# ScalarE's share of the mixer reordered, four decay banks, late gate weights, and the first tap of the K, V and Q tiles on VectorE

## The chip, the core and the metric

The kernel runs on one core of one Trainium2 chip. The metric is the device time of one launch in microseconds (us). It is written engine by engine: TensorE (PE in the profile), VectorE (DVE), ScalarE (ACT), GpSimd (POOL, only masks at the start) and the DMA queue of SyncE (SP) each run their own fixed list of instructions, and semaphores tie them together. An engine executes its list in order: a wait in it holds up everything behind it.

## The reference

Two layers, each of them a feed-forward block, a mixer, a second feed-forward block and a norm, on 512 tokens of width 1024 in float32. The change is in the mixer alone:

```python
def gated_deltanet_group(h, conv_w, a_log, dt_bias, out_g):
    qkv = jax.nn.silu(causal_depthwise_conv(h[..., Q0:Z0], conv_w))   # 4 taps, 12 tiles of 128 channels
    ...
    q = l2_normalize(qkv[:, :, 0]) * (GDN_HEAD_DIM ** -0.5)
    k = l2_normalize(qkv[:, :, 1])
    v = qkv[:, :, 2]
    ...
    g = -jnp.exp(a_log) * jax.nn.softplus(a + dt_bias)
    beta = jax.nn.sigmoid(b)
    o = chunk_gated_delta_rule(q, k, v, g, beta)    # 4 heads; decay exp(gc_i - gc_j); a triangular solve
    o = o * lax.rsqrt(jnp.mean(o * o, -1, keepdims=True) + NORM_EPS) * out_g
    return o * jax.nn.silu(z)

def conformer_conv_group(h, dw_w, dw_b, ln_g, ln_b):
    glu = h[..., G0:G0 + CONV_WIDTH] * jax.nn.sigmoid(h[..., G0 + CONV_WIDTH:IN_COLS])
    u = causal_depthwise_conv(glu, dw_w) + dw_b     # 31 taps, 4 tiles of 128 channels
    return jax.nn.silu(layer_norm(u, ln_g, ln_b))
```

## The kernel before

All large products keep float32 accuracy by splitting both operands: ScalarE rounds each 128x1024 piece of weights (`high`, L866, writes `wh`), VectorE subtracts to get the rest (`weight_low`, L1229, writes `wl`), and TensorE does three matmuls for one (L446 to L448). Such a piece is called a unit; a unit is 24 matmuls of 512 columns. There are four slots of weights: unit r+4 is loaded and prepared once unit r is done, `refill(r)` being VectorE's part.

The mixer of a layer goes in four stages.

1. **Input tiles.** Units 0 to 7 are the gated convolution's input. Units 8 to 19 are the twelve tiles of K (0 to 3), V (4 to 7) and Q (8 to 11). VectorE takes a tile out of its bank (`unit_out`, L1438, writes `pre`), which lets TensorE use the bank again three units on. ScalarE does the first of the four taps (`first_tap`, L1003, writes `cacc`), VectorE the other three (L1468), ScalarE the silu (`activate`, L1009) and, for K and Q, the square (L1012). Between these VectorE puts taps of the 31-tap convolution (`conv_taps`, L1393; 124 of them, wherever it would wait), shared out by the table `taps`. Inside this stage lie the gates: cumulated sums of g on TensorE, written to the bank `stat`; the squared norms of K; and the decay matrices, two matmuls (L637, L639) for each head into one of three banks, which ScalarE turns by an exponential into `Dm` (`decay`, L1025) and scales (`decay_scaled`, L1034).
2. **System.** TensorE forms K K for each head (L656) once its Q tile has left the bank, and Q K (L664) once VectorE has taken K K out (`system`, L1510). VectorE multiplies both by `Dm`. TensorE turns `Um` (L675) and sums the squares of Q (L614, one column each), ScalarE copies to `Tm`.
3. **Levels.** Six steps of a triangular inverse, for two pairs of heads each: TensorE L715, VectorE `pm` (L1536), TensorE L724, VectorE `Tm` (L1549), TensorE transposes (L733), ScalarE `Um` (L1099). In levels 1 to 4 TensorE and ScalarE also turn and scale V and K. VectorE fills in convolution taps.
4. **Chunks.** Four steps of a recurrence over the tokens, each of them a chain TensorE, ScalarE, TensorE, VectorE. The four gate units 20 to 23 (z) are cut into 32 pieces of 3 matmuls (`z_tiles`) that TensorE does in between. With them goes the layer norm of the convolution: the last taps, token sums (L453, `u`), the mean taken off (L1587), squares (L1120), token sums (L453, `glu`), a root, the factor spread over a bank (L474, `rcol`), the product (L1629), silu and split (L1130, L1133, L1634). Then the output units can start (`mix_out`).

## Time and profile before

| | |
|---|---|
| median of 3 runs | 2227.7 us (2221.02 to 2229.23) |
| the profiled execution's own time | 2227.2 us |
| its span, first to last instruction | 2225.5 us |
| busy: TensorE, VectorE, ScalarE | 2131.2, 1205.4, 720.2 us |
| mean granted clock of TensorE | 0.957 |

The profile has a page (busy times, the span in slices, the chain that ended last) and views that are read from the trace: waits (which instruction waited for which, in total), the timeline of an engine, and windows. All times of a timeline are counted from the span's start. Matmuls are pipelined, so TensorE counts as busy wherever it has work; how fast it works is told by the granted clock, 1.00 being full. Layer 0's mixer lies at about 412 to 697 us, layer 1's at 1504 to 1792; the second repeats the first 1092.2 us later to within a few hundredths until its end.

### The profile page before, as it was taken

To read this page: it belongs to the slowest core of one execution; us is meant where nothing else is said; L and a number is where in the kernel's file an instruction comes from. 1 tells how busy PE (TensorE), PEld (TensorE's weight loads), DVE (VectorE), ACT (ScalarE), POOL (GpSimd) and SP (SyncE) were. 2 spreads that over 40 slices of the span, in tenths; PEclk is the share of its full clock that TensorE was granted. 3 is DMA by queue.
4 is the path that set the end of the run, shared out by engine and by line. 5 is a ranking of instruction groups with operands and counts; after the bars stand their busy time and mean duration, and the time that the engine had idled before them with its cause. 6 is when DMAs were issued, how large, how long until landed. Compare 5 with 4: busy or idle time off the path is not lost.

```text
span 2225.5 us, 26379 instructions
## 1 busy us (share of the span) xinstructions
PE 2131.2 (96%) x10120; PEld 1788.6 (80%) x10120; DVE 1205.4 (54%) x1657; ACT 720.2 (32%) x998; POOL 5.9 (0%) x27
## 2 busy tenths in 40 slices
PE   7999999997998999999999999999979899999997
PEld 6888887786987788888788888877778778888886
DVE  5555423885764754542365553358768546555323
ACT  4222223354324422222342222234533343222222
POOL 1000000000000000000000000000000000000000
PEclk9999999997999999999999999999969799999997
DMA  5333333321002233333233333323200123333320
GB/s 159 102 94 94 97 96 91 86 76 38 1 19 76 74 96 99 99 87 98 80 95 95 94 92 97 100 66 100 67 20 1 38 68 95 94 94 94 102 78 38
DMA packets 345791, 177.53 MB, mean 80 GB/s; under 512 B 8338, under 2 KB 344692, under 8 KB 345716
## 3 DMA queue, kind: packets, MB, share of 16 engines
q1 hardware_dynamic: 344058, 176.34, 27.8%
q8 instruction: 50, 0.82, 0.2%
q10 hardware_dynamic: 1658, 0.16, 0.1%
q14 instruction: 25, 0.20, 0.0%
HBM read 174.38 MB, written 2.10 MB: 79 GB/s over the span
## 4 chain that ended last, share of the span: by engine, by line
PE 91%; DVE 5%; ACT 2%; issue 1%; DMA 0%; SPq 0%; DVEq 0%; ACTq 0%
PE res L446 24%; PE res L448 24%; PE res L447 24%; PE pq L715 2%; PE pq L724 2%; PE stat L453 2%; PE res L510 1%; DVE u L1393 1%; PE res L511 1%; PE pq L446 1%; PE res L514 1%; PE pq L448 1%; PE pq L447 1%; PE res L733 1%; PE bc L474 1%
## 5 line engine op out<-in xcount | busy, mean ns | idle before, releaser
L866 ACT ACTIVATE wh<-raw 128x1024 fp32r<-128x1024 f32 (+1 forms) x336 | 347.9, 1038 | 1036.3 <-PE res L448 1014.0
L446 PE MATMUL res<-xh,wh 128*128 128x512 f32 x1576 | 623.6, 396 | 5.3 <-DVE xl L1243 3.0
L448 PE MATMUL res<-xh,wl 128*128 128x512 f32 x1576 | 616.7, 391 | 0.0
L447 PE MATMUL res<-xl,wh 128*128 128x512 f32 x1576 | 616.5, 391 | 0.0
L1229 DVE TENSOR_TENSOR wl<-raw,wh 128x1024 fp32r<-128x1024 f32 (+1 forms) x336 | 401.5, 1197 | 392.2 <-ACT wh L866 391.7
L446 PEld LDWEIGHTS res<-xh,wh 128*128 128x128 f32 x1576 | 298.5, 189 | 68.7 <-ACT Um L1099 2.7
L448 PEld LDWEIGHTS res<-xh,wl 128*128 128x128 f32 x1576 | 297.7, 189 | 63.2
L447 PEld LDWEIGHTS res<-xl,wh 128*128 128x128 f32 x1576 | 298.4, 189 | 61.9 <-issue 1.4
L446 PE MATMUL res<-hh,wh 128*128 128x512 f32 x704 | 273.9, 389 | 0.0
L447 PE MATMUL res<-hl,wh 128*128 128x512 f32 x704 | 273.9, 389 | 0.0
L448 PE MATMUL res<-hh,wl 128*128 128x512 f32 x704 | 273.9, 389 | 0.0
L1318 DVE TENSOR_TENSOR us<-res,rs 128x512 f32<-128x512 f32 x84 | 58.0, 690 | 237.0 <-PE res L448 237.0
L1393 DVE SCALAR_TENSOR_TENSOR u<-glu,call,u 128x512 f32<-128x512 f32 x240 | 169.6, 744 | 0.3
L447 PEld LDWEIGHTS res<-hl,wh 128*128 128x128 f32 x704 | 132.1, 188 | 27.6
L448 PEld LDWEIGHTS res<-hh,wl 128*128 128x128 f32 x704 | 132.1, 188 | 27.4
L446 PEld LDWEIGHTS res<-hh,wh 128*128 128x128 f32 x704 | 132.1, 188 | 27.3
L1321 DVE TENSOR_TENSOR hf<-gs,us 128x512 f32<-128x512 f32 x88 | 61.0, 693 | 81.0 <-ACT gs L944 81.0
L1314 DVE TENSOR_TENSOR gs<-res,rs 128x512 f32<-128x512 f32 x84 | 58.0, 691 | 47.7 <-PE res L448 42.7
L1468 DVE SCALAR_TENSOR_TENSOR cacc<-pre,call,cacc 128x512 f32<-128x512 f32 x72 | 53.8, 747 | 32.5 <-ACT cacc L1003 30.2
L1323 DVE TENSOR_TENSOR hl<-hf,hh 128x512 f32 (+1 forms) x88 | 61.0, 693 | 8.7
L510 PE MATMUL res<-xh,wh 128*128 128x512 f32 x120 | 53.5, 446 | 11.4 <-ACT xh L887 11.4
L944 ACT ACTIVATE gs<-gs 128x512 f32<-128x512 f32 x88 | 54.1, 615 | 8.3 <-DVE gs L1314 8.2
(281 smaller groups left out, 1974.1 us busy)
## 6 DMA issues: line engine op xcount, KB each, us to landing
raw<-in_ffn_w_in SPq DMA_DIRECT2D x176, 512.0 KB, 3.8
raw<-in_ffn_w_out SPq DMA_DIRECT2D x64, 448.0 KB, 3.6
raw<-in_mix_w_in SPq DMA_DIRECT2D x48, 512.0 KB, 3.9
raw<-in_ffn_w_out SPq DMA_DIRECT2D x32, 512.0 KB, 3.8
raw<-in_mix_w_out SPq DMA_DIRECT2D x16, 512.0 KB, 3.8
xin<-in_x SPq DMA_DIRECT2D x4, 512.0 KB, 5.2
out_dram<-xin SPq DMA_DIRECT2D x4, 512.0 KB, 4.0
crows<-in_cm_dw_w ACTq DMA_DIRECT2D x1, 62.0 KB
```

The lines of the kernel that those rows point to most:

```text
L446: pe.matmul(bank, wh[:, slot, j, :], hi, start=first, stop=False)
L447: pe.matmul(bank, wh[:, slot, j, :], lo, start=False, stop=False)
L448: return pe.matmul(bank, wl[:, slot, j, :], hi, start=False, stop=last)
L510: pe.matmul(banks[n], wh[:, n, k, :], xh[:, k, :], start=k == 0, stop=False)
L866: act.activation(wh[:, slot, 0:nk, :], raw[:, slot, 0:nk, :], ACT.Copy).then_inc(hi_full, 1)
L944: act.activation(gs[:, odd, :], gs[:, odd, :], ACT.Silu).then_inc(silu_done, 1)
L1229: dve.tensor_tensor(wl[:, slot, 0:nk, :], raw[:, slot, 0:nk, :], wh[:, slot, 0:nk, :].bitcast(F32), ALU.subtract).then_inc(lo_full, 1)
L1314: dve.tensor_tensor(gs[:, odd, :], in_bank(unit_bank(r, 2 * f, l)), rs[:], ALU.mult).then_inc(gate_scaled, 1)
L1318: dve.tensor_tensor(us[:, odd, :], in_bank(unit_bank(r + 1, 2 * f, l)), rs[:], ALU.mult).then_inc(pair_free, 1)
L1321: ps.link(dve.tensor_tensor(hf[:], gs[:, odd, :], us[:, odd, :], ALU.mult))
L1323: dve.tensor_tensor(hl[:, p, :], hf[:], hh[:, p, :].bitcast(F32), ALU.subtract).then_inc(h_ready, 1)
L1393: ins = dve.scalar_tensor_tensor(u[:, t, :], src, w, u[:, t, :], ALU.mult, ALU.add)
```

## The change

The first tap goes from ScalarE to VectorE, as a plain product, and ScalarE's silu of a tile moves one tile later in its list. The gate sums get a copy in SBUF (`sums`), made by VectorE behind tile 6, so that `stat` is free to be a fourth decay bank; all four decays are then issued together, behind unit 17. The root of K's norms goes from ScalarE's tile 8 to its tile 7. The weights of the four gate units are prepared in levels 0 to 3 and not in tiles 8 to 11. Two of the four mean subtractions and six of the last eight gate pieces move.

```diff
+    sums = at("gate_sums", [P, 64], F32, o_gate + 128 * len(GN))
@@ TensorE
-                    bank = three[h % 3]
+                    bank = turned[h]
...
-                mixer_units(16, 17)
-                decays(0)
-                decays(1)
-                mixer_units(17, 18)
-                decays(2)
-                mixer_units(18, 19)
-                pe.wait_ge(d_exp, l * H + 1)
-                decays(3)
-                mixer_units(19, 20)
+                mixer_units(16, 18)
+
+                pe.wait_ge(sums_out, l + 1)
+                for h in range(H):
+                    decays(h)
+                mixer_units(18, 20)
...
-                z_tiles(4)
                 for t in range(CT):
                     pe.wait_ge(usq_ready, l * CT + t + 1)
                     mm = token_sums(glu[:, t, PADC:], first=t == 0, last=t == CT - 1)
                 mm.then_inc(vsum_full, 1)
-                z_tiles(4)
+                z_tiles(2)
                 pe.wait_ge(udiag, l + 1)
                 spread_column(rcol).then_inc(uvbc_full, 1)
+                z_tiles(6)
@@ ScalarE
                     n = r - 2 * CT
-                    first_tap(n)
+                    if n:
+                        activate(n - 1)
...
-                    high(MBASE + r + SLOTS, r % SLOTS, 8, l)
+                    if n < 2 * H:
+                        high(MBASE + r + SLOTS, r % SLOTS, 8, l)
...
-                    activate(n)
-                    if n == 3:
+                    if n == 4:
                         softplus()
-                    if n == 8:
-                        act.wait_ge(l2_full, l + 1)
-                        act.wait_ge(gc_full, l + 1)
-                        act.activation(gt["ss"][:, 0:16], stat[:, 128:144], ACT.Sqrt,
+                    if n == 7:
+                        act.wait_ge(sums_out, l + 1)
+                        act.activation(gt["ss"][:, 0:16], sums[:, 32:48], ACT.Sqrt,
                                        bias=eps[:, 0:1]).then_inc(l2_root, 1)
...
+                    if n == 9:
...
                         for h in range(H):
                             decay(h)
-                    if n == 9:
+                    if n == 10:
                         decay_scaled(0)
                         decay_scaled(1)
-                    if n == 10:
+                    if n == 11:
                         decay_scaled(2)
                         decay_scaled(3)
+                activate(3 * H - 1)
...
                 for n in range(6):
+                    if n < H:
+                        high(MBASE + Z_U + n, n, 8, l)
@@ VectorE
                     unit_out(r, pre[:, PADG:])
-                    conv_taps(first)
-                    dve.wait_ge(tap0_ready, l * 3 * H + n + 1)
+                    dve.wait_ge(mix_free, l * MIX_IN_U + r + 1)
+                    if n >= 2:
+                        dve.wait_ge(act_kvqz, l * 4 * H + n - 1)
...
+                        if k == 0:
+                            mark = st.done(dve.tensor_scalar(cacc[:, n % 2, :], pre[:, 0:T], w, None, ALU.mult))
+                            conv_taps(first)
+                            continue
...
+                            elif n < 2 * H:
+                                refill(r)
                             else:
-                                refill(r)
+                                conv_taps(1)
...
-                taps = [(1, 1, 1), (1, 1, 1), (1, 1, 0), (1, 1, 1),
-                        (1, 1, 1), (1, 1, 0), (1, 0, 0), (1, 0, 0),
-                        (1, 1, 0), (1, 1, 1), (1, 1, 1), (1, 1, 0)]
+                taps = [(1, 1, 1), (1, 1, 1), (1, 0, 0), (1, 1, 0),
+                        (1, 1, 0), (1, 0, 0), (1, 0, 0), (1, 0, 0),
+                        (1, 1, 0), (1, 1, 1), (1, 1, 1), (1, 0, 0)]
...
+                    if n == 6:
+                        dve.wait_ge(gc_full, l + 1)
+                        dve.tensor_copy(sums[:], stat[:, 96:160]).then_inc(sums_out, 1)
-                    if n == 9:
+                    if n == 8:
                         dve.wait_ge(l2_root, l + 1)
...
-                        conv_taps(2)
+                        conv_taps((3, 2)[g])
+                    if n < H:
+                        weight_low(MBASE + Z_U + n, n, 8, l)
...
-                        conv_taps((2, 3)[g])
+                        conv_taps((3 if n >= H else 2, 2)[g])
...
                     if c == 3:
                         o_sum(1)
                         refill(Z_U + 1)
-                        dve.wait_ge(mubc_full, l + 1)
-                        for t in range(CT):
+                        for t in range(2, CT):
                             dve.tensor_tensor(u[:, t, :], u[:, t, :], bc[:, :], ALU.subtract).then_inc(uc_ready, 1)
...
                     if c == 2:
                         o_sum(0)
                         z_unit(1)
+                        dve.wait_ge(mubc_full, l + 1)
+                        for t in range(2):
+                            dve.tensor_tensor(u[:, t, :], u[:, t, :], bc[:, :], ALU.subtract).then_inc(uc_ready, 1)
```

The first place is ScalarE's list in the mixer around tile 8, from the root of K's norms (`gate_ss`) on. Before:

```order
L1060 ACT_TABLE_LOAD
L1060 ACTIVATE gate_ss<-stat,eps 128x16
L1062 ACT_TABLE_LOAD
L1062 ACTIVATE gate_egc<-stat 128x16
L1063 ACTIVATE gate_egl<-stat 128x16
L1064 ACTIVATE gate_ekd<-stat 128x16
L1025 ACTIVATE Dm<-pq 128x512 x2
L1025 ACTIVATE Dm<-bc 128x512
L1025 ACTIVATE Dm<-pq 128x512
L1003 ACTIVATE cacc<-pre,call 128x512
L866 ACTIVATE wh<-raw 128x1024
L1009 ACT_TABLE_LOAD
```

And now:

```order
L1054 ACTIVATE gate_ss<-gate_sums,eps 128x16
L1002 ACT_TABLE_LOAD
L1002 ACTIVATE vT<-cacc 128x512
L1002 ACTIVATE qT<-cacc 128x512
L1005 ACTIVATE ksqQ<-qT 128x512
L1057 ACT_TABLE_LOAD
L1057 ACTIVATE gate_egc<-gate_sums 128x16
L1058 ACTIVATE gate_egl<-gate_sums 128x16
L1059 ACTIVATE gate_ekd<-gate_sums 128x16
L1018 ACTIVATE Dm<-pq 128x512 x2
L1018 ACTIVATE Dm<-bc 128x512
L1018 ACTIVATE Dm<-stat 128x512
```

The tap row `cacc<-pre,call` of tile 9 stood behind the root, two table loads and the exponentials (three small ones for the gates, four for the decays); now no row of ScalarE writes `cacc`, the root stands alone ahead of the last V tile's silu (`vT`), and the mixer's list has one table load more in each layer.

The second place is VectorE's list in level 1, from the `pm` of the first pair of heads to the `Tm` of the second and what follows it (`u` rows are convolution taps). Before:

```order
L1536 TENSOR_TENSOR pm<-pq,lmask 128x512
L1393 SCALAR_TENSOR_TENSOR u<-glu,call,u 128x512 x2
L1536 TENSOR_TENSOR pm<-pq,lmask 128x512
L1393 SCALAR_TENSOR_TENSOR u<-glu,call,u 128x512 x2
L1549 TENSOR_TENSOR Tm<-Tm,pq 128x128x4
L1393 SCALAR_TENSOR_TENSOR u<-glu,call,u 128x512 x2
L1549 TENSOR_TENSOR Tm<-Tm,pq 128x128x4
L1393 SCALAR_TENSOR_TENSOR u<-glu,call,u 128x512 x3
```

The same stretch now:

```order
L1541 TENSOR_TENSOR pm<-pq,lmask 128x512
L1391 SCALAR_TENSOR_TENSOR u<-glu,call,u 128x512 x3
L1541 TENSOR_TENSOR pm<-pq,lmask 128x512
L1391 SCALAR_TENSOR_TENSOR u<-glu,call,u 128x512 x2
L1227 TENSOR_TENSOR wl<-raw,wh 128x1024
L1556 TENSOR_TENSOR Tm<-Tm,pq 128x128x4
L1391 SCALAR_TENSOR_TENSOR u<-glu,call,u 128x512 x2
L1556 TENSOR_TENSOR Tm<-Tm,pq 128x128x4
L1391 SCALAR_TENSOR_TENSOR u<-glu,call,u 128x512 x2
```

Between the first `pm` and the second `Tm` stand one tap and one weight row more; behind it one tap less.

## Rows read from the trace of the kernel before

**Rows 1.** The page: the span, and each engine's busy time.

```profile
span 2225.5 us, 26379 instructions
PE 2131.2 (96%) x10120; PEld 1788.6 (80%) x10120; DVE 1205.4 (54%) x1657; ACT 720.2 (32%) x998; POOL 5.9 (0%) x27
```

**Rows 2.** Waits, both layers: who waited for whom, total us, times, longest.

```profile
DVE cacc L1468 <- ACT cacc L1003: 30.2, 8, 7.5
...
PE res L656 <- DVE pre L1438: 13.2, 2, 6.6
PE res L446 <- DVE loc L1634: 13.2, 2, 6.6
...
PE res L664 <- ACT qT L1009: 10.9, 2, 5.5
```

**Rows 3.** Timeline of TensorE in the system stage, layer 0: start, us, instruction, [idle before].

```profile
517.89 2.89 PE L656 MATMUL res<-kT 128*128 128x128 f32 x24
527.37 2.07 PE L656 MATMUL res<-kT 128*128 128x128 f32 x8 [6.59 <-DVE pre L1438]
534.90 3.75 PE L664 MATMUL res<-qT,kT 128*128 128x128 f32 x16 [5.45 <-ACT qT L1009]
...
544.57 1.84 PE L614 MATMUL stat<-ones,ksqQ 128*128 128x1 f32 x16
...
547.59 0.75 PE L715 MATMUL pq<-Tm,Bm 128*128 128x64 f32 x3 [0.69 <-ACT Tm L1076]
```

**Rows 4.** Timeline of ScalarE, layer 0: two unit ends, and tile 8.

```profile
428.70 1.06 ACT L866 ACTIVATE wh<-raw 128x1024 fp32r<-128x1024 f32 x1 [2.30 <-PE res L448]
434.14 1.06 ACT L866 ACTIVATE wh<-raw 128x1024 fp32r<-128x1024 f32 x1 [4.38 <-PE res L448]
...
504.39 1.28 ACT L1060 ACT_TABLE_LOAD   x1
...
512.61 0.60 ACT L1025 ACTIVATE Dm<-pq 128x512 f32<-128x512 f32 x1 [3.53 <-PE pq L639]
```

**Rows 5.** Timeline of VectorE, layer 0: input tiles, and the start of the system.

```profile
421.49 1.00 DVE L1389 TENSOR_SCALAR u<-glu,call 128x512 f32<-128x512 f32 x2
...
432.60 4.06 DVE L1393 SCALAR_TENSOR_TENSOR u<-glu,call,u 128x512 f32<-128x512 f32 x6
...
513.85 0.75 DVE L1468 SCALAR_TENSOR_TENSOR cacc<-pre,call,cacc 128x512 f32<-128x512 f32 x1 [7.49 <-ACT cacc L1003]
...
526.63 0.68 DVE L1438 TENSOR_TENSOR pre<-res,rs 128x512 f32<-128x512 f32 x1
...
534.07 0.68 DVE L1510 TENSOR_TENSOR Bm<-res,Dm 128x512 f32<-128x512 f32 x1
```

**Rows 6.** Timeline of VectorE: the first `pm` of levels 0, 1 and 5.

```profile
551.15 0.69 DVE L1536 TENSOR_TENSOR pm<-pq,lmask 128x512 f32<-128x512 f32 x1 [4.81 <-PE pq L715]
...
566.64 0.69 DVE L1536 TENSOR_TENSOR pm<-pq,lmask 128x512 f32<-128x512 f32 x1 [2.57 <-PE pq L715]
...
607.18 0.69 DVE L1536 TENSOR_TENSOR pm<-pq,lmask 128x512 f32<-128x512 f32 x1 [1.32 <-PE pq L715]
```

**Rows 7.** Windows: stretch, busy times, then PEclk (granted clock), DMA share, GB/s.

```profile
535.00:541.00 6.00, 6.00 (x28) 5.92 (x29) 5.18 (x11) 1.07 (x2) 0.00 (x0) 0.50 0.30 87
548.00:564.00 16.00, 16.00 (x77) 16.00 (x77) 8.73 (x14) 0.90 (x1) 0.00 (x0) 0.50 0.00 1
...
1759.00:1766.00 7.00, 7.00 (x28) 6.13 (x28) 0.75 (x4) 1.17 (x3) 0.00 (x0) 0.54 0.01 2
```

**Rows 8.** Timeline at the end of the chunks, layer 0, three engines.

```profile
654.86 0.69 DVE L1576 TENSOR_TENSOR Xd<-pq,gate_egc 128x512 f32<-128x512 f32 x1 [0.57 <-PE pq L759]
...
663.62 2.17 ACT L1120 ACTIVATE glu<-u 128x512 f32<-128x512 f32 x4
...
665.13 3.63 PE L453 MATMUL stat<-ones,glu 128*128 128x1 f32 x32
...
671.75 0.69 DVE L1438 TENSOR_TENSOR zT<-res,rs 128x512 f32<-128x512 f32 x1 [2.30 <-PE res L448]
```

More of the change, by code:

```diff
@@ L628, in _ @@
                 pe.matmul(stat[:, 112:128], ones[:], gt["g"][:, 0:16], start=True, stop=True)
-                pe.matmul(stat[:, 160:176], lowst[:], gt["g"][:, 0:16], start=True, stop=True).then_inc(gc_full, 1)
+                pe.matmul(stat[:, 144:160], lowst[:], gt["g"][:, 0:16], start=True, stop=True).then_inc(gc_full, 1)
                 def decays(h):
-                    bank = three[h % 3]
+                    bank = turned[h]
                     if h == 0:
@@ L998, in _ @@
                 row_out(2, 1, l)
-                def first_tap(n):
-                    w0 = C_QKV + (1, 2, 0)[n // H] * H + n % H
-                    act.wait_ge(mix_free, l * MIX_IN_U + 2 * CT + n + 1)
-                    act.activation(cacc[:, n % 2, :], pre[:, 0:T], ACT.Copy,
-                                   scale=call[:, l, w0:w0 + 1]).then_inc(tap0_ready, 1)
                 def activate(n):
@@ L1024, in decay @@
                     act.wait_ge(e_full, l * H + h + 1)
-                    act.activation(Dm[:, h], three[h % 3].rearrange("p (c t) -> p c t", c=NC),
+                    act.activation(Dm[:, h], turned[h].rearrange("p (c t) -> p c t", c=NC),
                                    ACT.Exp).then_inc(d_exp, 1)
@@ L1460, in qkv @@
                     unit_out(r, pre[:, PADG:])
-                    conv_taps(first)
-                    dve.wait_ge(tap0_ready, l * 3 * H + n + 1)
-                    mark = 0
-                    for k in range(1, GTAPS):
+                    dve.wait_ge(mix_free, l * MIX_IN_U + r + 1)
+                    if n >= 2:
+                        dve.wait_ge(act_kvqz, l * 4 * H + n - 1)
+                    for k in range(GTAPS):
                         w = call[:, l, C_QKV + k * 3 * H + which * H + n % H:C_QKV + k * 3 * H + which * H + n % H + 1]
-                        if k > 1:
-                            st.need(mark)
+                        if k == 0:
+                            mark = st.done(dve.tensor_scalar(cacc[:, n % 2, :], pre[:, 0:T], w, None, ALU.mult))
+                            conv_taps(first)
+                            continue
+                        st.need(mark)
                         ins = dve.scalar_tensor_tensor(cacc[:, n % 2, :], pre[:, k:k + T], w, cacc[:, n % 2, :],
@@ L1531, in _ @@
                 scores(H - 1)
+                dve.wait_ge(br_ready, l + 1)
+                dve.wait_ge(ekd_ready, l + 1)
+                dve.tensor_tensor(gt["kd"][:, 0:16], gt["br"][:, 0:16], gt["ekd"][:, 0:16],
+                                  ALU.mult).then_inc(kd_ready, 1)
                 conv_taps(2)
```

21 lines of the change are left out of this document (9 added, 12 removed).

## The prediction

> **What bounds the kernel now.** The page first [rows 1]: TensorE is busy 96% of the span, so only what stands in TensorE's way, or slows its clock, is worth anything; VectorE at 54% and ScalarE at 32% matter only where TensorE waits for them. The waits come next [rows 2]: TensorE stands 13.2 us for VectorE's tile `pre` and 10.9 us for the silu `qT`, in two waits each, so once in each layer, and 13.2 us for `loc` at the end of the mixer. VectorE stands 30.2 us for ScalarE's first tap. Third, the timelines. TensorE finishes unit 19 and the K products of three heads by 520.8, then stands 6.59 us, does eight matmuls and stands 5.45 us [rows 3]. What is late is VectorE: its wait of 7.49 us for the first tap of tile 9 ends at 513.85, tile 11 leaves its bank at 526.63, the system starts at 534.07 [rows 5]. What held ScalarE is in rows 4: the root's table load at 504.39, then the fourth decay, which had no bank until the first was read (3.53 us), and only then the tap. Fourth, the windows [rows 7]: the granted clock is 0.50 (1.2 GHz) in 535 to 541, behind the idle stretch, and again in 548 to 564, level 0, behind two bursts of one-column matmuls, the second at 544.57 [rows 3].
>
> **The first tap on VectorE and the end of the tap wait.** Durations of VectorE overlap by some 0.09 us: six three-operand taps take 4.06, so 0.66 each; two tensor-scalar products take 1.00, so 0.46 each [rows 5]; a tensor-tensor of 0.69 counts 0.60; an instruction that needs the one just ahead starts 0.13 later. The new first tap is such a product of the same shape, 0.46. Its bounds are 0.46 and 0.66, and I take 0.46, the same form. TensorE is not slowed in the tiles: everything up to unit 17 runs as before, and it needs nothing from VectorE that is younger than two or three tiles. So unit 19 still ends at 517.9 [rows 3]. A unit takes 5.44, the distance of two passes that wait for unit ends [rows 4], and as all decays now stand ahead of unit 18, that one ends at 512.5. VectorE is at tile 10 by then and waits for it. Tile 10 is 0.73 (take out, result needed), 0.46, and seven operations of 0.66: 5.8, so tile 11 leaves its bank at 518.3. Tile 11 is 0.73 + 0.46 + five operations of 0.66 or 0.79, 3.4 in all: 4.6. The system starts at 522.9 and not at 534.07, **11.1 us earlier**. ScalarE keeps up: unit 17 ends at 502.7 (512.5 less a unit and some 4.3 for four decays, each a unit's fifth), the decays end by 506.9 and their exponentials by 509; the silu and square of tile 10 end at 519.0, the last eight scalings, 0.3 each, at 521.4, and the third head needs them only at 525.6. The bound below is unit 19's end plus 4.6, 522.5; the bound above 524.9, with 0.2 more for each of the ten remaining operations. TensorE's idle stretch shrinks from 6.59 + 5.45 to some 2.3 us.
>
> **One table load more.** It is 1.28 us long [rows 4] and stands between the root and the silu of tile 7. ScalarE is through with it at about 495.6, and that silu waits for VectorE until 497.5: I count 0. Were that cover gone, it would be 1.28 in each layer, 2.6 together.
> The Trainium skill (ScalarE: Activation LUTs, "What ACT_TABLE_LOAD costs") speaks against the change here: a switch costs 2.66 us with its drain, 5.3 us for two. By the page the sum below would be 2220.5 if nothing covered it. The row agrees with the load itself (1.28 us) and shows nothing of a drain.
>
> **The system stage.** Between 534.07 and level 0 at 547.59 lie 13.5 us [rows 3, 5], partly at 1.2 GHz. At 2.4 GHz eight matmuls of 128 columns take 0.9 and not the 1.9 of half of 3.75. From the system's start VectorE's list then sets the pace to the second Q K product, turned tile 1 ends at 5.6, a burst of one-column matmuls at 7.3, the fourth Q K at 8.2, a turned tile at 8.7, the second burst (1.7) at 10.4, the last turned tile at 10.9, and ScalarE's copy of it and the wait of 0.69 [rows 3] make 11.6: **1.9 us less**. Lower bound 0.
>
> **The levels.** `pm` of level 1 to `pm` of level 5 is 40.54 us, 10.13 a level [rows 6], and TensorE sets it: VectorE has idle time ahead of each `pm` (1.32). Now VectorE has from the first `pm` to the end of the second `Tm` 0.60 + 3 taps + 0.60 + 2 taps + 1.13 (a weight pass) + 0.60 + 2 taps + 0.69 = 8.3, taps at 0.66. Then TensorE transposes the second pair (0.9) and multiplies for the next level (1.9): 11.1. So VectorE becomes the bound in levels 1 to 3 and each costs 1.0 more; level 4, with an extra tap and no weights, is 7.8 + 2.8 = 10.6, 0.5 more; in level 5 the way to the end grows from 6.5 to 7.8, 1.3 more. Level 0, 15.5 us from `pm` to `pm` [rows 6], is slow enough at 1.2 GHz to hide it all. Sum **4.7 us more**; bounds 0 (if taps slip into waits) and 4.7 + 1.0.
>
> **The chunks.** The convolution's 124 taps are given out by tables: ahead of the chunks 22 with its own input, 27 in the tiles (23 by the table, 4 in place of refills; before 28), 2 behind the system, 56 in the levels (before 54), so 107 (before 106), then 14 in the first two steps, so the last burst, on which the token sums wait, is 3 taps and not 4: **0.7 less**. At their end it turns: two mean subtractions stand ahead of the fourth `Xd`. VectorE had 0.57 of idle time there [rows 8] and now is 0.55 late. TensorE does its 2 pieces by 663.0 and then waits for the squares, the first of which is ready at 664.2 + 0.6 [rows 8], where before it did four more pieces until 665.13. From the sums' end (3.5 us later, 668.3) eight pieces (5.44) and a spread (0.9) follow before the last gate tile can leave its bank, and that tile stands in VectorE's list ahead of the products, silus and `loc` for which TensorE waits. It left at 671.75 [rows 8]; now it leaves at 674.7, **2.95 us later**. Bounds 0 and 2.95 + 3.2 (below).
>
> **Sum.** -11.1 - 1.9 + 4.7 - 0.7 + 3.0 = -6.0 us in a layer, -12.0 in both: 2227.2 - 12.0 = 2215.2 by the profiled execution's own time, which is 1.7 over its span and 0.5 under the median of the runs. I say **2215**.
>
> **Rivals.**
> *Level 0 keeps its full clock.* For it: the idle stretch ahead of it is mostly gone, and only one of four runs of before is 6 us faster than the rest, as if the slow stretch came and went. Against: the one-column bursts and the wait of 0.69 behind them stay as they are, and before, the clock had recovered by 541 and fell at 548 all the same. Then level 0 takes 11.2 and not 17.2 from its first matmul: 5.9 less in a layer, 2209 for one, 2203 for both.
> The Trainium skill (TensorE: Matmul & The Clock Gate, "What's actually happening") has the lower clock as the state that sustained activity lifts and idleness brings back. By that rule the removal of 9.7 us of idleness would bring this rival. The trace agrees for 535 to 541 and not for 548 to 564, where TensorE was busy throughout.
> *The clock falls at the norm's sums.* Layer 1 has it now: granted 0.54 in 1759 to 1766 [rows 7], 6.4 us at half speed, so 3.2 lost; layer 0 has not. The new order puts 1.9 us of idleness ahead of these sums. Layer 0 would lose 3.2: 2218.
> *VectorE is no faster for it.* It has 24 more operations, and if the tiles ran at its pace with 0.66 for each, or a silu held a buffer, half of the 11.1 would be gone: 2226. Against: all its waits for ScalarE's tap go, 7.49 in tile 9 alone [rows 5].
> *Late weights, slower.* In levels 0 to 3 ScalarE's pass stands ahead of its copies, and VectorE's in the middle of the bound chain. If the raw piece came late, each level would stand, at worst a unit's pace, 5.44 [rows 4], four times: +21.8 in a layer, 2259. It decides against the change from 1.5 us a level on (6.0 over four). Against: the slots are freed in tiles 4 to 7, more than 20 us ahead.
>
> **Chances.** The forecast (2211 to 2219) 0.40; full clock in one or both level 0 (2203 to 2211) 0.30; clock lost at the sums (about 2218) 0.15; half of the gain gone 0.10; late weights 0.05. Leaving out the last and most of the one before gives 2203 to 2221. A change under 0.5% (11 us, so 2216.6) is about what this measurement cannot tell from none: faster gets all of the second case, two thirds of the first and a little of the third, 0.60; same 0.35; slower 0.05.
>
> **What the new profile would show.** No wait of VectorE for `cacc` of ScalarE; the first system product about 11 us earlier, TensorE's waits ahead of L656 gone; `pm` to `pm` 11.1 in levels 1 to 3, with VectorE as the releaser of a transpose; the last gate tile taken out 19.3 us behind the fourth `Xd` (674.7 less 655.4), where it was 16.9 (671.75 less 654.86) [rows 8]; a clock of 0.50 in level 0 or not. I would be wrong if `pre` of tile 10 were taken well after unit 18's end, or if level 0 ran at 2.4 GHz.

## The result, and the profile after

The changed kernel took 2213.1 us, median of 4 runs (2210.35 to 2217.77), and the kernel before, in runs on the same chip, 2228.3 (2221.02 to 2229.23, 4 runs). The ratio is 0.9941, 95% interval 0.9914 to 0.9968: 0.6% faster. The profiled execution took 2210.35 for a span of 2208.6, which is 16.9 us less than before [rows 1].

The page of the changed kernel, span and busy times:

```profile
span 2208.6 us, 26401 instructions
...
PE 2117.0 (96%) x10120; PEld 1773.6 (80%) x10120; DVE 1214.7 (55%) x1683; ACT 707.2 (32%) x976; POOL 6.0 (0%) x27
```

TensorE has the same 10120 instructions and 14 us less of busy time: the same work at a higher mean granted clock, 0.966 where it was 0.957. The waits of the changed kernel, in the columns of [rows 2]:

```profile
DVE zT L1436 <- PE res L450: 15.4, 2, 7.7
...
PE res L448 <- DVE loc L1643: 15.0, 2, 7.5
PE res L732 <- DVE Tm L1556: 14.5, 20, 1.5
...
PE stat L455 <- DVEq L1614: 4.6, 2, 2.3
PE res L663 <- ACT qT L1002: 4.5, 2, 2.3
...
PE stat L455 <- ACT glu L1118: 3.5, 2, 1.7
```

VectorE's 30.2 us for the tap and TensorE's 13.2 for `pre` are gone, and its 10.9 for `qT` are 4.5. New are VectorE's two waits of 7.7 for the last gate tile, `zT`, TensorE's twenty short waits for `Tm` in the levels, 14.5 us together where the list of before has 0.6, and its two of 1.7 ahead of the norm's sums (`glu`). The wait for `loc` has grown from 13.2 to 15.0. The 4.6 ahead of the first token sums (those of `u`) are not new: they were 5.9. TensorE in the system stage of layer 0, where [rows 3] had it:

```profile
517.83 3.73 PE L655 MATMUL res<-kT 128*128 128x128 f32 x32
523.81 3.62 PE L663 MATMUL res<-qT,kT 128*128 128x128 f32 x16 [2.25 <-ACT qT L1002]
...
532.51 1.84 PE L616 MATMUL stat<-ones,ksqQ 128*128 128x1 f32 x16
...
535.53 3.79 PE L714 MATMUL pq<-Tm,Bm 128*128 128x64 f32 x32 [0.69 <-ACT Tm L1072]
```

VectorE, the same layer: the last tile, the system's start, `pm` of levels 0, 1, 2 and 5, and the last `Tm`:

```profile
518.42 0.68 DVE L1436 TENSOR_TENSOR pre<-res,rs 128x512 f32<-128x512 f32 x1
...
522.98 0.69 DVE L1511 TENSOR_TENSOR Bm<-res,Dm 128x512 f32<-128x512 f32 x1
...
537.57 0.69 DVE L1541 TENSOR_TENSOR pm<-pq,lmask 128x512 f32<-128x512 f32 x1 [3.20 <-PE pq L714]
...
549.72 0.69 DVE L1541 TENSOR_TENSOR pm<-pq,lmask 128x512 f32<-128x512 f32 x1 [2.49 <-PE pq L714]
...
560.90 0.69 DVE L1541 TENSOR_TENSOR pm<-pq,lmask 128x512 f32<-128x512 f32 x1 [1.59 <-PE pq L714]
...
593.94 0.69 DVE L1541 TENSOR_TENSOR pm<-pq,lmask 128x512 f32<-128x512 f32 x1 [1.59 <-PE pq L714]
...
601.04 0.69 DVE L1556 TENSOR_TENSOR Tm<-Tm,pq 128x512 f32<-128x512 f32 x1
```

Windows of layer 0, in the columns of [rows 7]: the start of the system stage, level 0, and the norm's sums:

```profile
524.00:527.00 3.00, 3.00 (x15) 3.00 (x15) 2.36 (x6) 0.39 (x1) 0.00 (x0) 0.50 0.00 0
...
545.00:547.00 2.00, 1.71 (x9) 1.31 (x8) 2.00 (x4) 1.02 (x1) 0.00 (x0) 0.50 0.76 222
...
654.00:660.00 6.00, 6.00 (x23) 5.42 (x23) 0.93 (x4) 1.34 (x3) 0.00 (x0) 0.50 0.02 4
```

The half clock of the system stage and of level 0 is now 3.4 us each (windows of 1 us from 523 and from 544), where it was 17.1 each; that at the sums, 6.8 us long, is new in this layer. The end of the chunks, VectorE and TensorE, against [rows 8]:

```profile
642.75 0.69 DVE L1583 TENSOR_TENSOR Xd<-pq,gate_egc 128x512 f32<-128x512 f32 x1
...
651.65 5.18 PE L455 MATMUL stat<-ones,glu 128*128 128x1 f32 x32 [1.73 <-ACT glu L1118]
...
665.19 0.69 DVE L1436 TENSOR_TENSOR zT<-res,rs 128x512 f32<-128x512 f32 x1 [7.67 <-PE res L450]
...
671.73 2.49 DVE L1643 TENSOR_TENSOR loc<-u,hic 128x512 fp32r<-128x512 f32 x4
```

Added up, in us from one event to the next (`Wm` is VectorE's first operation behind the mixer's gate; the second column of each pair is layer 1):

| stretch | before | after | difference |
|---|---|---|---|
| up to the system's start `Bm` (for layer 1, without what layer 0 had brought) | | | -11.1, -11.3 |
| `Bm` to `pm` of level 1 | 32.6, 32.6 | 26.7, 26.7 | -5.8, -5.9 |
| that `pm` to the last `Tm` | 46.3, 46.3 | 51.3, 51.3 | +5.0, +5.0 |
| last `Tm` to the fourth `Xd` | 41.9, 41.9 | 41.7, 41.8 | -0.2, -0.1 |
| fourth `Xd` to the last `zT` | 16.9, 20.1 | 22.4, 22.4 | +5.5, +2.4 |
| `zT` to `Wm` | 13.2, 13.4 | 13.2, 13.2 | -0.1, -0.2 |
| sum | | | -6.7, -10.1 |

### The profile page after: what moved, and what is told of

Read it like the earlier page. It is cut to its first block, busy times and chain, and to the rows that moved or that the text cites. A ratio compares the mean times of both kernels' runs of the same rounds, so it can differ in the third digit from the quotient of the medians.

```text
span 2208.6 us, 26401 instructions
## 1 busy us (share of the span) xinstructions
PE 2117.0 (96%) x10120; PEld 1773.6 (80%) x10120; DVE 1214.7 (55%) x1683; ACT 707.2 (32%) x976; POOL 6.0 (0%) x27
## 4 chain that ended last, share of the span: by engine, by line
PE 88%; DVE 9%; ACT 2%; issue 1%; DMA 0%; SPq 0%; DVEq 0%; ACTq 0%
PE res L448 24%; PE res L449 24%; PE res L450 24%; DVE u L1391 3%; PE stat L455 2%; PE res L512 1%; PE res L513 1%; PE pq L448 1%; PE res L516 1%; PE pq L449 1%; PE pq L450 1%; PE pq L714 1%; PE bc L476 1%; DVE pm L1541 1%; PE res L732 1%
```

## The experiments

Twelve kernels ran, in jobs in which the kernel before had medians of 2225.5 to 2228.0.

**The tap alone.** The kernel before, with only the first tap moved to VectorE:

```diff
-                    first_tap(n)
...
+                    mark = st.done(dve.tensor_scalar(cacc[:, n % 2, :], pre[:, 0:T], call[:, l, w0:w0 + 1], None,
+                                                     ALU.mult))
                     conv_taps(first)
-                    dve.wait_ge(tap0_ready, l * 3 * H + n + 1)
```

> The kernel before with the first tap on VectorE and nothing else moved: gate weights stay in tiles 8 to 11, three decay banks, ScalarE's root and exponentials still in tile 8. Theory (the tap's wait was only where ScalarE's late list showed): VectorE no longer stands in tile 9, but it stands in tiles 10 and 11 for ScalarE's rounding of the weights, which comes behind the same exponentials; the system of layer 0 starts at about 530 us, 4 us earlier than the 534.07 of before and 7 later than the 522.98 of the changed kernel, and the time is 2228 - 8 = about 2220 us. Rival (the tap on VectorE is what brought the 11 us): system at 524 or earlier, 2228 - 22 = 2206 us or a little over, since the levels keep their 10.1.

Measured: 2199.8 us (2197.75 to 2208.46, 4 runs), ratio 0.9898 (0.9871 to 0.9926). VectorE in layer 0:

```profile
514.01 1.23 DVE L1229 TENSOR_TENSOR wl<-raw,wh 128x1024 fp32r<-128x1024 f32 x1 [5.31 <-ACT wh L866]
...
529.16 0.68 DVE L1513 TENSOR_TENSOR Bm<-res,Dm 128x512 f32<-128x512 f32 x1
...
543.88 0.69 DVE L1539 TENSOR_TENSOR pm<-pq,lmask 128x512 f32<-128x512 f32 x1 [3.29 <-PE pq L715]
...
553.34 0.69 DVE L1539 TENSOR_TENSOR pm<-pq,lmask 128x512 f32<-128x512 f32 x1 [0.94 <-PE pq L715]
```

The mechanism was as my theory had it: VectorE is held by ScalarE's list one step later (5.31 us for the weight `wh` of tile 9), and the system starts at 529.16, 4.9 earlier than before and 6.2 later than in the changed kernel. The time was not. The kernel with the worse start is 13 us faster than the whole change by the medians (10 by the two ratios; 12.6 between the profiled executions). Against the changed kernel, layer 0: +6.2 at `Bm`, +0.1 to level 0, -2.7 in level 0 (9.46 from `pm` to `pm`, where the changed kernel has 12.15), -5.0 in the levels, +0.2 in the chunks, -4.4 at their end, -0.7 behind: -6.2 from `Wm` to `Wm` (the rounded terms give 6.3). So in layer 0 the rest of the change wins 6.2 us at the start and gives 12.4 back, 2.7 of them by the clock of level 0.

**The tap back.** The changed kernel, with the first tap on ScalarE again:

```diff
+                    if n >= 2:
+                        act.wait_ge(act_kvqz, l * 4 * H + n - 1)
+                    first_tap(n)
                     if n:
                         activate(n - 1)
...
-                            mark = st.done(dve.tensor_scalar(cacc[:, n % 2, :], pre[:, 0:T], w, None, ALU.mult))
                             conv_taps(first)
+                            dve.wait_ge(tap0_ready, l * 3 * H + n + 1)
```

> The changed kernel with the first tap given back to ScalarE, at the head of each tile's turn in its list, everything else as changed. Theory (the order of ScalarE's list, with the fourth bank and the weights gone from tiles 8 to 11, brought the 11 us): the system of layer 0 starts within 1 us of 522.98 and the time is within 3 us of the changed kernel's 2213. Rival (the tap on VectorE brought it): VectorE waits for the tap again in tiles 9 to 11, the system starts at 528 or later, 2223 us or more.

Measured: 2221.8 us (2219.72 to 2226.13, 10 runs), ratio 0.9989 (0.9978 to 1.0). VectorE, tile 8 and the system's start:

```profile
501.99 0.69 DVE L1445 TENSOR_TENSOR pre<-res,rs 128x512 f32<-128x512 f32 x1
...
526.50 0.68 DVE L1518 TENSOR_TENSOR Bm<-res,Dm 128x512 f32<-128x512 f32 x1
```

From tile 8 to `Bm` are 24.5 us, as in the changed kernel (498.48 to 522.98), and 36.4 before (497.70 to 534.07); with the tap alone 31.0. So the order of ScalarE's list, not the tap, takes the wait out of tiles 8 to 11; the two remedies overlap. The 3.5 us later start is made before tile 8, and level 0 takes 15.2 from `pm` to `pm` in both layers, 3 us more than in the changed kernel. Neither forecast came true as it stood: the system starts 3.5 us later than the theory had it, and 1.5 earlier than the rival.

**The end of the chunks as before.** The changed kernel with TensorE's and VectorE's lists at the end of the chunks as they were:

```diff
+                z_tiles(4)
                 for t in range(CT):
                     pe.wait_ge(usq_ready, l * CT + t + 1)
...
-                z_tiles(2)
+                z_tiles(4)
                 pe.wait_ge(udiag, l + 1)
                 spread_column(rcol).then_inc(uvbc_full, 1)
-                z_tiles(6)
...
```

> The changed kernel with the end of the chunks as before: four gate pieces ahead of the norm's sums and four behind, all four mean subtractions in the last step. Theory (the new order delays the last gate tile, for which the whole end of the mixer waits): the tile leaves 16.9 us behind the fourth Xd product and not 22.4, TensorE does not stand ahead of the sums, the clock does not fall there in layer 0; 3 us less a layer and up to 3 more for the clock, 2213 - 6 to 12 = 2201 to 2207 us. Rival (the six pieces cover TensorE's later wait for loc, as its wait is where the time goes): the same 2213 or slower.

Measured: 2203.0 us (2198.8 to 2204.64, 4 runs), ratio 0.9897 (0.9875 to 0.992), 10 us under the changed kernel. Layer 0:

```profile
642.59 0.69 DVE L1583 TENSOR_TENSOR Xd<-pq,gate_egc 128x512 f32<-128x512 f32 x1 [0.57 <-PE pq L758]
...
652.87 4.52 PE L455 MATMUL stat<-ones,glu 128*128 128x1 f32 x32
...
662.65 0.69 DVE L1436 TENSOR_TENSOR zT<-res,rs 128x512 f32<-128x512 f32 x1 [4.57 <-PE res L450]
```

The last gate tile leaves its bank 20.1 us behind the fourth `Xd`, in layer 1 18.4, where the changed kernel has 22.4 in both. That is 6.4 of the 10 us; the rest is level 0 (11.3 us in layer 0, where it was 12.15) and the clock in blocks that the edit doesn't touch, which I did not follow. The theory had 16.9 and a full clock at the sums of layer 0. TensorE indeed doesn't stand ahead of them (652.87, no idle time), but the clock falls there all the same, for 6.8 us from 655 (windows of 1 us). So the idle piece ahead of these sums is not what it takes for the clock to fall at them.

**The last gate tile late.** The changed kernel, its order at the end of the chunks kept, with the last gate tile taken out behind `loc` on VectorE. With it go ScalarE's rounding pass for the same unit, which moves behind the norm's silus, and TensorE's wait for the tile, which moves to the second output unit:

```diff
+                    if m == 1:
+                        pe.wait_ge(mix_free, l * MIX_IN_U + MIX_IN_U)
                     if m == 0:
-                        pe.wait_ge(mix_free, l * MIX_IN_U + MIX_IN_U)
+                        pe.wait_ge(mix_free, l * MIX_IN_U + MIX_IN_U - 1)
...
-                z_refill(3)
...
+                z_refill(3)
...
-                z_unit(3)
                 refill(Z_U + 2)
...
+                z_unit(3)
                 refill(Z_U + 3)
```

> The changed kernel with one thing moved: the last gate tile leaves its bank behind the loc subtractions and not ahead of the norm's products, on VectorE; ScalarE's rounding pass that waits for the same unit goes behind the norm's silus; TensorE waits for that tile from the second output unit on. Theory (that tile stands in the chain only by VectorE's order): the products start as soon as the factor is spread, 7 to 9 us earlier, TensorE's wait of 7.5 us ahead of the output units falls under 2 us, 8 us less a layer, about 2197 us. Rival (the chain is set by the sums, root and spread): the wait for loc stays above 5 us and the time within 4 us of 2213.

Measured: 2197.2 us (2190.88 to 2203.02, 4 runs), ratio 0.9871 (0.984 to 0.9902), with level 0 at half clock in both layers. Layer 0:

```profile
646.04 0.68 DVE L1585 TENSOR_TENSOR Xd<-pq,gate_egc 128x512 f32<-128x512 f32 x1
...
668.86 2.50 DVE L1644 TENSOR_TENSOR loc<-u,hic 128x512 fp32r<-128x512 f32 x4
671.27 0.69 DVE L1438 TENSOR_TENSOR zT<-res,rs 128x512 f32<-128x512 f32 x1
```

`loc` comes 22.8 us behind the fourth `Xd`; it was 29.0 in the changed kernel and 23.4 and 26.6 in that before. From `loc` to `Wm` are 4.6 us where they were 6.6. So the end of the mixer is 8.1 us shorter in each layer, 16.2 together, and level 0 with its lost clock takes 3 us of that back in each: the profiled execution (2198.58) is 11.8 us under that of the changed kernel, and the medians differ by 16. The cost was the place of the tile, ahead of `loc`; VectorE's list, ScalarE's pass and TensorE's wait were moved together and not tried apart.

**The weights back in the tiles.** The changed kernel, with both engines' passes over the gate weights in tiles 8 to 11 again, four refills in the place of taps, and none in the levels:

```diff
-                    if n < H:
-                        weight_low(MBASE + Z_U + n, n, 8, l)
...
```

> The changed kernel with the four gate weight units prepared in tiles 8 to 11 again (ScalarE's and VectorE's pass in each; the four refills take the place of the taps there, and the weights' passes leave the levels). My account of the changed kernel: a weight pass of VectorE (1.13 us) inside the bound chain of a level makes levels 1 to 3 cost 11.17 us and not the 10.13 of before. Expected then: pm to pm 10.1 in levels 1 to 3 (3 us less in a layer), and the passes, about 1.1 us of ScalarE and 1.1 of VectorE each, come back ahead of the system, where only tile 10 and 11 are VectorE's chain: system start 2.3 us later (525.3). Net -1 to -2 us in a layer, 2209 to 2211. Rival (the longer levels come of the taps, 3 and 2 in place of 2 and 2, and not of the weights): pm to pm stays 11.1 or falls by no more than 0.3, the system is 2.3 later all the same, 2217. Second rival (the weights' place sets TensorE's clock: in the kernel before and in the one with the first tap alone the system stage was longer): the start later by 2.3 gives the idle stretch back, and level 0 is at half clock for 17 us, +3 to +6 in a layer, 2217 to 2223.

Measured: 2214.2 us (2211.06 to 2216.14, 6 runs), ratio 0.995 (0.9933 to 0.9967): no change, between the theory's 2209 to 2211 and the rivals' 2217. `pm` of levels 1 and 2, layer 0:

```profile
550.06 0.69 DVE L1539 TENSOR_TENSOR pm<-pq,lmask 128x512 f32<-128x512 f32 x1 [1.59 <-PE pq L714]
...
560.20 0.69 DVE L1539 TENSOR_TENSOR pm<-pq,lmask 128x512 f32<-128x512 f32 x1 [1.70 <-PE pq L714]
```

A level is 10.1 again, so the weight pass was the 1.0 that each level had cost; levels 4 and 5, which have a tap more and no weights, stay at 10.7 and 7.1. The system starts at 525.09, 2.1 later, as said. The gain of 3 is nearly taken back by this, and layer 1 has its level 0 at 15.1 from `pm` to `pm`.

**The weights behind the levels.** VectorE's pass behind the second `Tm`, out of the bound chain, the taps as 2, 2 and 2, 3, and the two taps left over in the chunks:

```diff
-                        conv_taps((3, 2)[g])
-                    if n < H:
-                        weight_low(MBASE + Z_U + n, n, 8, l)
+                        conv_taps(2)
...
-                        conv_taps((3 if n >= H else 2, 2)[g])
+                        conv_taps((2, 3)[g])
+                    if n < H:
+                        weight_low(MBASE + Z_U + n, n, 8, l)
...
-                    conv_taps((5, 4, 0, 0)[c])
+                    conv_taps((7, 4, 0, 0)[c])
```

> The changed kernel with VectorE's pass over the gate weights moved, in levels 1 to 4, from ahead of the first update of Tm to behind the second, so out of the chain between pm and the last Tm, and with the taps of a level given out as 2, 2 and 2, 3, where it had 3, 2 and 2, 2 with the weight pass between (the two taps left over stand in the chunks' first burst, 7 in place of 5). My account: levels 1 to 4 are 11.2, 11.2, 11.2 and 10.7 us because VectorE's list from pm to the second Tm is one weight pass and one tap longer, so all return to 10.1 to 10.2, and level 5 to 6.5: 5 us less in a layer, last Tm 5 us earlier, the rest of the program shifted by as much; 2203. Rival (ScalarE's pass over the same weights, which stands ahead of its copies of the turned tiles, is what holds the levels): pm to pm stays at 11.1, no change, 2213. Rival 2 (the raw weights land late): VectorE's pass waits for ScalarE's in the new place too, and the level's first pm comes late; 10.7 a level, 2208.

Measured: 2201.2 us (2192.75 to 2201.64, 4 runs), ratio 0.9898 (0.9875 to 0.992). `pm` of levels 2 and 3 and the last `Tm`, layer 0:

```profile
558.29 0.69 DVE L1541 TENSOR_TENSOR pm<-pq,lmask 128x512 f32<-128x512 f32 x1 [0.18 <-PE pq L714]
...
568.43 0.69 DVE L1541 TENSOR_TENSOR pm<-pq,lmask 128x512 f32<-128x512 f32 x1 [0.18 <-PE pq L714]
...
594.48 0.68 DVE L1554 TENSOR_TENSOR Tm<-Tm,pq 128x512 f32<-128x512 f32 x1
```

10.1 a level, with the same weights in the same levels. What counted was not the work but whether it stood between `pm` and `Tm`. From `pm` of level 1 to the last `Tm` are 46.2 us in both layers, 5.1 less than in the changed kernel; the last edit puts 3.1 of these down to the weights, and the rest is the taps of levels 4 and 5. The profiled execution is the fastest of the four, 2192.75 at a mean granted clock of 0.970, with level 0 at full clock in both layers (9.6); the others took 2200.84 to 2201.64 at 0.965. So the clock also differs between executions of one kernel, and a profile shows one of them.

**Both places mended.** The last edit and the late gate tile together.

> The changed kernel with two edits together: VectorE's pass over the gate weights behind the levels' updates (as in the run sent with it), and the last gate tile taken out behind loc rather than ahead of it (as in the run of the last batch, 2197.2). If the two costs stand at different places and add, it takes their sum: 5 us in a layer from the levels and 8 from the end of the mixer, 2213 - 10 - 16 = 2187. Rival (the levels' delay was hidden by other work, or what is gained there is lost again to a stretch of half clock, as the granted clock falls for 3 to 17 us at level 0 in some kernels and not in others): no better than the one edit alone, 2197, or up to 2203 with level 0 at half clock.

Measured: 2183.8 us (2180.62 to 2185.54, 4 runs), ratio 0.9821 (0.9799 to 0.9844). The two costs add. But `pm` of levels 0 and 1, in layer 0 and in layer 1 of the same execution:

```profile
535.03 0.69 DVE L1543 TENSOR_TENSOR pm<-pq,lmask 128x512 f32<-128x512 f32 x1 [3.32 <-PE pq L714]
...
550.29 0.69 DVE L1543 TENSOR_TENSOR pm<-pq,lmask 128x512 f32<-128x512 f32 x1 [1.21 <-PE pq L714]
...
1609.54 0.69 DVE L1543 TENSOR_TENSOR pm<-pq,lmask 128x512 f32<-128x512 f32 x1 [3.20 <-PE pq L714]
...
1619.12 0.68 DVE L1543 TENSOR_TENSOR pm<-pq,lmask 128x512 f32<-128x512 f32 x1
```

Level 0 takes 15.3 us in layer 0 and 9.6 in layer 1, for the same instructions.

**Tap alone and late gate tile.** The kernel before with the first and the fourth edit.

> The kernel before with two edits only: the first tap on VectorE (2199.8 alone) and the last gate tile taken out behind loc. It has none of the changed kernel's other parts. Its end of chunks is the old one, whose sums are not late: with the tap alone the last gate tile leaves its bank 18.1 us behind the fourth Xd and loc comes 24.6 behind it. Expected if the tile stands in loc's way here too: loc 22 us behind the fourth Xd, 2 to 3 us less in a layer, 2195; the stretch of half clock behind the mixer may shrink too, 3 more, 2190. Rival (in the old order the tile is in nobody's way, since the silus and loc wait for TensorE's spread anyway): loc at 24.6, 2200.

Measured: 2204.5 us (2194.66 to 2206.67, 4 runs), ratio 0.99 (0.9866 to 0.9934), not told apart from the tap alone. `loc` comes 25.7 and 24.1 us behind the fourth `Xd`, with the tap alone 24.6 and 24.9. In the old order the tile is in nobody's way; the rival held.

**The clock of level 0.** Three runs ask what makes it fall. In the first two the kernel before is the base; first Q's sums are left out:

```diff
-                q_norms(0)
-                q_norms(1)
                 scores(3)
                 turn_u(2)
-                q_norms(2)
-                q_norms(3).then_inc(q2_full, 1)
...
```

> The kernel before with work left out: the two bursts of one-column matmuls that sum the squares of Q in the system stage (2 x 8 rows of 4 passes, 1.84 us of TensorE each) are gone, and the scale of the output norm is made from K's sums in their place, so the output is not the reference's. Everything else is as before. Theory (the bursts ahead of level 0 make the granted clock fall, as each of TensorE's other stretches of half clock in a busy time stands behind one-column matmuls or an idle stretch): level 0 at full clock in both layers, pm to pm 9.5 us where it was 15.5, and the system stage 2 to 3 us shorter; 2226 - 12 - 5 = 2209. Rival (the fall comes of the whole system stage, its waits and short transposes, or of something that comes and goes): pm to pm 15.4 in one or both layers, and only the bursts' own 3.7 us a layer at most are gained: 2219 to 2222.

Measured: 2207.5 us (2202.72 to 2213.35, 4 runs), ratio 0.9913 (0.9884 to 0.9943). The window of level 0:

```profile
548.00:558.00 10.00, 9.61 (x87) 9.37 (x87) 8.82 (x15) 2.05 (x2) 0.00 (x0) 1.00 0.01 2
```

Full clock in both layers, 9.46 from `pm` to `pm`, although the idle pieces ahead of the system and their half clock (17.1 and 13.7 us) stayed. By itself this is weak evidence: the kernel with the tap alone also had 9.46 in both layers, with its bursts. Then the same sums, moved into level 0 in place of the system stage:

```diff
                         if g == 0 and 1 <= n < 5:
                             turn_tile(2 * n - 1)
+                        elif n == 0:
+                            q_norms(g + 1)
...
```

> The kernel before with the sums of Q's squares moved, nothing left out: four matmuls of one column at a time, between the products and transposes of level 0, in place of the two bursts in the system stage. If the bursts' being together is what lets the clock fall: level 0 at full clock, 9.5 + 1.8 = 11.3 us pm to pm where it was 15.5, system stage 2 to 3 us shorter; 2226 - 2 x 6.7 = 2213. If one-column matmuls anywhere near do it, or the stage does: level 0 at half clock, pm to pm 15.5 to 18, the system stage shorter by 2 to 3 all the same: 2220 to 2226.

Measured: 2248.2 us (2246.24 to 2251.09, 4 runs), ratio 1.0094 (1.0073 to 1.0114): 20 us slower than before, and far outside what both theories gave. Windows of levels 0 and 1:

```profile
548.00:564.00 16.00, 16.00 (x78) 16.00 (x78) 7.58 (x12) 1.02 (x1) 0.00 (x0) 0.50 0.00 1
564.00:586.00 22.00, 22.00 (x109) 22.00 (x109) 8.80 (x14) 5.36 (x11) 0.00 (x0) 0.51 0.01 1
```

TensorE is busy for all of these 38 us and has half its clock in both layers (37.5 us each), where before it had it for 17.1. The last of the sums ends at 564, and the clock stays at half for 22 us more. Scattering the one-column matmuls made it worse. The same move on the kernel with both places mended:

> The kernel with both places mended (2183.8 in the last batch; level 0 at half clock for 13.7 us in one of its two layers, pm to pm 15.3 and 9.6) with the same move of the sums of Q's squares into level 0. If it keeps the clock: level 0 is 11.3 in both layers, on average 1.1 us shorter than the mean of 15.3 and 9.6, and the system stage is 1 to 2 us shorter: 2183.8 - 2 x 2.6 = 2178 to 2180. If the clock falls whatever stands there: 2183 to 2187.

Measured: 2205.1 us (2198.24 to 2210.77, 4 runs), ratio 0.9912 (0.9886 to 0.9937), 21 us over the kernel that it changes, and again outside what both readings gave (2178 to 2187). From level 0 on it has 34.1 us of half clock in layer 0, into level 1, and 17.1 in layer 1.

**Wide sums.** So the last run left the sums where they were and made them wide, on the kernel with both places mended:

```diff
-                        mm = pe.matmul(stat[:, n:n + 1], squares[:, h, c * P:(c + 1) * P], ones[:, 0:1], start=True,
-                                       stop=True)
+                        mm = pe.matmul(stat[:, n:n + 64], squares[:, h, c * P:(c + 1) * P], ones[:, 0:64],
+                                       start=True, stop=True)
```

> The kernel with both places mended (2183.8) and one edit more: each matmul that sums the squares of K or Q over a head takes 64 columns of ones in place of one. The next matmul overwrites 63 of them, so what is read is the same, at the same places of the program. The rows of other runs put a 64-column matmul at 0.118 us (32 in 3.79) and a one-column one at 0.107 to 0.115 (16 in 1.84, 32 in 3.63), so the width costs 0.2 us a burst at most. Theory (it is the one column that lets the granted clock fall, not the place, the waits or the length of the bursts): no stretch of 0.50 behind K's sums in the tiles, 3.4 to 6.8 us there now, which is 1.7 to 3.4 us lost; none in level 0, pm to pm 9.5 to 9.6 in both layers where it was 15.3 and 9.6; the stretch of 3.4 behind the idle piece ahead of the Q K products stays. 2183.8 - 5 - 5.7 + 1 = 2174. Rival (the idle pieces and short transposes of the stages do it, and the kernel without the Q sums only had no burst at all): the clock falls at the same places, 2183 to 2185.

Measured: **2172.1 us** (2170.32 to 2173.34, 5 runs), ratio 0.9751 (0.9734 to 0.9767). The second burst, layer 0:

```profile
530.55 1.90 PE L616 MATMUL stat<-ones,ksqQ 128*128 128x64 f32 x16
```

The window behind K's sums in the kernel before:

```profile
477.00:482.00 5.00, 5.00 (x14) 4.03 (x14) 4.87 (x9) 2.30 (x3) 0.00 (x0) 0.50 0.38 107
```

And in this one, behind K's sums and in level 0, of layer 0 and of layer 1:

```profile
474.00:484.00 10.00, 10.00 (x62) 8.86 (x61) 7.85 (x16) 5.49 (x9) 0.00 (x0) 1.00 0.40 105
534.00:546.00 12.00, 11.61 (x106) 11.37 (x105) 10.38 (x17) 3.89 (x6) 0.00 (x0) 1.00 0.01 2
...
1549.00:1555.00 6.00, 6.00 (x32) 5.05 (x31) 5.93 (x10) 1.87 (x3) 0.00 (x0) 1.00 0.08 12
...
1600.00:1612.00 12.00, 11.61 (x106) 11.37 (x105) 11.45 (x18) 4.14 (x7) 0.00 (x0) 1.00 0.04 11
```

The burst takes 1.90 us where it took 1.84, the clock is 1.00 at all four places, and `pm` to `pm` of level 0 is 9.57 in both layers. The strongest comparison is at K's sums: in the profiles of all thirteen kernels that sum K's squares one column wide, the changed kernel and the one before among them, the clock falls at or behind these sums in both layers, for 3.4 to 10.2 us, and here it doesn't in either. For level 0 the profile alone would say less, since with the bursts of one column in the system stage 8 of 20 levels 0 kept the full clock too. But all five runs lie within 3 us of each other, at a mean granted clock of 0.973 to 0.975, where those of the kernel before span 10.5.

## Why the prediction was right, and where not

The forecast was 2215 and the median 2213.1. The start of the system, the levels and the end of the chunks came out in their order and nearly in their size. But two terms were off by more than the total was, and with opposite signs, so that the total came out within 2 us is in part luck: the profiled execution lost 16.9 us, where the sum had 12.0.

- *System start.* Forecast 522.9, -11.1; measured 522.98, and no wait for the tap. What I took for the work of the tap was mostly that of ScalarE's order: either alone gives 4.9 (tap) or 7.6 (order), both 11.1.
- *Table load.* Counted at 0, and right at the place: `pre` of tile 8 leaves its bank at 498.48, 0.8 later than before, and the system starts to 0.1 us where it was forecast. The silu behind the load waited for VectorE until 497.39. No drain beside the load shows in the traces either: in the kernel before, the load takes 1.28 us from 504.39 and ScalarE's next instruction starts at 505.69. The further load was not tried by itself.
- *System stage.* Forecast -1.9 from `Bm` to level 0; measured 12.55 (522.98 to 535.53) where it was 13.52, so -1.0. The term was mis-sized: TensorE waits for `qT` until 523.81 and then does the first 16 rows of products at half clock, 3.62 us, as before (3.75).
- *Level 0.* Forecast no change; measured 12.15 where it was 15.49, and with the part ahead of its first `pm` 4.9 less in layer 0 and 4.8 in layer 1. This is the first rival, nearly in full (it was priced at 5.9), and the prediction's own sign of being wrong, level 0 at 2.4 GHz, came about but for 3.4 us. The forecast's step "the one-column bursts and the wait of 0.69 behind them stay as they are" was true and didn't decide. Over the runs with these bursts in place `pm` to `pm` of level 0 was anything from 9.5 to 15.5, and different in two layers of one execution, so no change of this kind has a fixed price here. That the sums of one column have a part in it is shown by the last runs: with the sums scattered the half clock lasts longer, and with both K's and Q's sums 64 wide it is gone at K's sums and in level 0, and the runs no longer spread. What lets the clock through with narrow sums in some executions, as in the changed kernel, stays open.
- *Levels.* Forecast +4.7, measured +5.0 (11.2 in levels 1 to 3). The weight pass in the chain is shown to be the 1.0 a level by the run that put it back into the tiles; VectorE is the releaser of the transposes, as forecast (14.5 us of waits for `Tm`).
- *End of the chunks.* The 0.7 from one tap less and the 0.55 by which the fourth `Xd` was to be late leave 0.15 less up to that `Xd`; measured 0.2 and 0.1 less. Forecast +2.4 from there to the last gate tile with the clock as before. Layer 1, which had the half clock already, shows +2.4. Layer 0 shows +5.5, because the clock now falls at the norm's sums there too (654 to 660): the second rival, whose 3.2 is the 3.1 over. I left this out of the sum on too little ground; the idle piece of 1.73 us ahead of the sums that I had worked out (1.9) is in the trace. But it isn't shown to be the cause: the clock fell at these sums without any idle time ahead of them in layer 1 of the kernel before (from 1759; the sums start at 1757.31) and in layer 0 of the run with the old order.
- *Sum.* -6.0 in a layer was forecast, -6.7 and -10.1 measured. Layer 0's extra of level 0 and its loss at the sums nearly cancel (-4.9 and +3.1); in layer 1 the sums' loss was there before, and the gain of level 0 stays.

The rival of late weights gave nothing: no level waits for them. But the levels and the end of the chunks together cost 7 to 10 us in a layer. In the levels this stands in the list of waits only as twenty pieces of at most 1.5 us; at the end of the chunks a good part of it is work at half clock, in which TensorE stays busy and which no list of waits shows.

The Trainium skill (TensorE: Matmul & The Clock Gate, "What's actually happening") has the lower clock as what comes after idleness. That holds for the stretches behind the idle pieces here (524 to 527, behind 2.25 us). It doesn't hold in the profile's own sense of idle for level 0: TensorE was busy for all of 548 to 564 before [rows 7] and for 38 us in the run with scattered sums, at 0.50 to 0.51.

## What to carry to other kernels

A change of several parts should be run part by part: here one part alone was 13 us faster than all of them, and with the two losses mended the whole was 29 us faster than as it was made. Work that is moved "where the engine has time" belongs behind the operation that others wait for, not ahead of it; two places of VectorE's list were worth 16 and 12 us, with what the clock did in those runs and two moved taps included. Where TensorE is busy and its clock still falls, look at what it was given to do before, and give one-column matmuls more columns if they cost the same.

## What the runs showed of the hardware

- A matmul of one column, of 64 and of 128 take nearly the same here at full clock: 16 rows in 1.84 us, 16 in 1.90, and 32 of the K K products in 3.73. With the sums of K's and Q's squares 64 columns wide the granted clock was 1.00 behind K's sums in both layers and in level 0 of layer 0, where the same kernel with one column had 0.50; that alone brought 11.7 us (2183.8 to 2172.1).
- One-column matmuls between others, 16 in a level, went with a clock of 0.50 for 37.5 us with TensorE busy throughout, and cost 20 us. At K's sums in the kernel before it was 0.50 in 477 to 482 with TensorE busy for all of it.
- The same instructions can have full clock in one layer and half clock in the other, in one execution (9.6 and 15.3 us), and one kernel can have different clocks from one execution to the next (2192.75 us at 0.970, 2201 at 0.965). What decides it stays open. The token sums of the norms still have one column, and in layer 0 of the fastest kernel three stretches of half clock, 10.2, 6.8 and 6.8 us by windows of 1 us, stand at or behind them; whether width would keep the clock there was not tried.
